# A one-column square root ahead of the last-tile wait in every RMS norm

## What is computed

```
def rms_norm(x, g):
    return x * rsqrt(mean(x*x, axis=-1) + EPS) * g
def ada_norm(x, g, shift, scale):
    return rms_norm(x, g) * (1 + scale) + shift

for layer in 0, 1:
    x += 0.5 * gate * swiglu(ada_norm(x, ...))          # FFN
    x += gate * mixer(ada_norm(x, ...))                 # layer 0: S5 scan, layer 1: gated DeltaNet
    x += 0.5 * gate * swiglu(ada_norm(x, ...))          # FFN
return rms_norm(x, final_g)
```

## Time and profile before

| | |
|---|---|
| median of 3 runs | 2415.01 us |
| lowest, highest | 2410.72, 2417.9 us |
| span of the profiled execution | 2416.0 us |
| TensorE matmul busy | 2139.0 us (89%), 12486 instructions |
| VectorE busy | 1612.0 us (67%) |
| GpSimd busy | 752.2 us (31%) |
| ScalarE busy | 703.8 us (29%), 992 instructions |

### The profile page before, as it was taken

The page is one execution under the profiler, slowest core; times in us unless marked ns, Lnnn a source line. Parts: engine busy times, 40 slices in busy tenths (PEclk is TensorE's granted clock), DMA queues, the critical chain, the costliest instruction groups (busy, mean ns, idle before and its releaser), DMA issues.

```text
span 2416.0 us, 34067 instructions
## 1 busy us (share of the span) xinstructions
PE 2139.0 (89%) x12486; PEld 1810.0 (75%) x12486; DVE 1612.0 (67%) x2255; ACT 703.8 (29%) x992; POOL 752.2 (31%) x588
## 2 busy tenths in 40 slices
PE   3898998982889899999799999869999999788997
PEld 0676777762878588887588888668888888778997
DVE  7867785853434885858885853637777777746555
ACT  1311221221133321212331212324344344324432
POOL 2144663742524120202311212303333223323123
PEclk9999999995679899999999999869999999988999
DMA  7354553639943344444353532211111111003553
GB/s 281 112 219 167 200 196 134 222 126 205 280 127 122 127 169 157 174 140 176 109 201 122 181 132 78 82 35 36 35 35 35 35 35 34 1 18 122 185 181 105
DMA packets 104689, 309.62 MB, mean 128 GB/s; under 512 B 27680, under 2 KB 39456, under 8 KB 95136
## 3 DMA queue, kind: packets, MB, share of 16 engines
q1 hardware_dynamic: 89392, 285.80, 35.3%
q10 hardware_dynamic: 12528, 12.33, 1.7%
q0 software_dynamic: 2688, 10.42, 1.1%
HBM read 280.26 MB, written 28.25 MB: 128 GB/s over the span
## 4 chain that ended last, share of the span: by engine, by line
PE 60%; issue 16%; DVE 10%; POOL 8%; DMA 2%; ACT 1%; SPq 1%; DVEq 1%; ACTq 0%; POOLq 0%
PE PS L219 18%; PE PS L220 17%; PE PS L221 17%; POOL EE L1877 2%; DVE wlo L252 1%; PE PS L1154 1%; POOL DTs L1867 1%; DVE t L920 1%; POOL X L1873 1%; DMA vwS<-vwd 1%; DVE bx L921 1%; PE PS L585 1%; DVE bx L919 1%; DVE rstd L358 1%; PE PS L1027 1%
## 5 line engine op out<-in xcount | busy, mean ns | idle before, releaser
L219 PE MATMUL PS<-hh,whi 128*128 128x512 f32 (+1 forms) x1792 | 662.0, 369 | 46.2 <-DVE hl L376 38.5
L221 PE MATMUL PS<-hh,wlo 128*128 128x512 f32 (+1 forms) x1792 | 653.3, 365 | 0.0
L220 PE MATMUL PS<-hl,whi 128*128 128x512 f32 (+1 forms) x1792 | 653.1, 364 | 0.0
L252 DVE TENSOR_TENSOR wlo<-raw,whi 128x1024 fp32r<-128x1024 f32 x328 | 493.4, 1544 | 94.5 <-ACT whi L246 91.5
L219 PEld LDWEIGHTS PS<-hh,whi 128*128 128x128 f32 x1792 | 342.6, 191 | 124.6 <-issue 56.0
L246 ACT ACTIVATE whi<-raw 128x1024 fp32r<-128x1024 f32 x328 | 329.0, 1051 | 319.7 <-PE PS L221 303.6
L221 PEld LDWEIGHTS PS<-hh,wlo 128*128 128x128 f32 x1792 | 343.1, 191 | 53.1
L220 PEld LDWEIGHTS PS<-hl,whi 128*128 128x128 f32 x1792 | 343.9, 192 | 49.8
L566 POOL CAST hidh<-gt 128x512 f32 (+2 forms) x88 | 59.8, 680 | 905.9 <-DVE gt L515 905.9
L219 PE MATMUL PS<-hidh,whi 128*128 128x512 f32 (+1 forms) x704 | 263.4, 374 | 37.1 <-DVE x L551 26.0
L220 PE MATMUL PS<-hidl,whi 128*128 128x512 f32 (+1 forms) x704 | 260.5, 370 | 0.0
(11 more groups left out here) (298 smaller groups left out, 2946.2 us busy)
## 6 DMA issues: line engine op xcount, KB each, us to landing
modw<-in_mod_w SPq DMA_DIRECT2D x72, 1024.0 KB, 4.8
raw<-in_w_gdn SPq DMA_DIRECT2D x32, 512.0 KB, 4.0
cxd<-cx POOLq DMA_DIRECT2D x16, 576.0 KB, 4.4
cxS<-cxd SPq DMA_DIRECT2D x8, 1152.0 KB, 5.9
raw<-in_w_f0p0a SPq DMA_DIRECT2D x16, 512.0 KB, 6.9
vwd<-vws ACTq DMA_DIRECT2D x16, 512.0 KB, 6.8
raw<-in_w_f0p1a SPq DMA_DIRECT2D x16, 512.0 KB, 6.6
raw<-in_w_glu SPq DMA_DIRECT2D x16, 512.0 KB, 4.2
```

The source lines that it names most:

```text
L219: pe.matmul(dst, w_h, xh, start=first, stop=False)
L220: pe.matmul(dst, w_h, xl, start=False, stop=False)
L221: return pe.matmul(dst, w_l, xh, start=False, stop=last)
L252: dve.tensor_tensor(wlo[:, s, c], raw[:, s, c], whi[:, s, c].bitcast(F32), ALU.subtract)\
```

## The change

Every `norm_act` gets two instructions ahead of its wait for the last tile of `x`: a wait for `mods_ready` to be at least 1 (that is, for `epst` to be written), and a `Sqrt` of the one column of `epst` into a new tile `root_warm` that nothing reads.

```diff
         epst = sb("epst", [P, 1])
+        root_warm = sb("root_warm", [P, 1])
         glub = sb("glub", [P, 2, KT])
...
         def norm_act(act, m):
             layer, n, c0, feeds = NORMS[m] if m < len(NORMS) else (0, 0, CTX, "out")
+            act.wait_ge(mods_ready, 1)
+            act.activation(root_warm[:, :], epst[:, 0:1], ACT.Sqrt)
             if m:
                 for q in range(2):
                     act.wait_ge(x_ready[q], 1 + X_BEFORE[m])
```

## The result

The changed kernel takes 2442.08 us (median of 4 runs, 2441.09 to 2446.06) against 2415.93 us of the kernel before beside it: a ratio of 1.011, 95% interval 1.009 to 1.013. That is 26 us slower where 0.5 us faster was forecast. The profiled execution agrees: its span is 2440.3 us, 24.3 more than the 2416.0 before.

What follows compares the result with a forecast made beforehand. The kernel was taken as bound by matmuls, TensorE carrying 60% of the chain; gains of 0.10, 0.09, 0.10 and 0.22 us summed to 0.51, so 2415.01 - 0.5 = 2414.5 us. The range was 2409.5 to 2419.5 us.

Steps and rivals of the forecast that it cites:

- D: Shift's loop at line 316: a table load in each pass, 18 us slower in all, 2433 us; chance 0.03.
- The norms: Roots of norms 1, 3, 4 and 6 start earlier by 0.10, 0.09, 0.10 and 0.22 us, sum 0.51; others nothing.
- upper bound of 1.7 us: Most the norms could gain if two 512-column matmuls took 0.74 us: 3 x 0.48 + 0.22 us.
- norm 2's idle time: ScalarE ahead of norm 2's square: some 1.0 us idle left after load and root, in place of 2.51.
- norm 0's root: Norm 0: square later, at about 44.5 us, but root where it was, covered by 12.7 us.
- rival B: Norms where the load ended last: the whole load comes off in four, 5.1 us, giving 2409.9 us; chance 0.03.
- its cover: Norm 2: load and root end 1.0 us before the square; 1.5 us lost if this fails.

Runs made afterwards that it cites:

- root_no_tile: Kernel before plus the seven early roots and waits, the root written to a second column of `epst` instead of a new tile; 2416.76 us, ratio 0.9997.
- tile_only: Kernel before plus an unused 4-byte tile declared behind `epst`, with no root and no wait; 2439.47 us, ratio 1.010.
- the sweep: Separate matmul-only kernel, not a change to either kernel, stepping the distance between moving operand and weights; 0.2267 us at 0 bytes, 0.2333 at 32 (512 columns).
- root_two_tiles: Changed kernel plus a second, unused tile declared behind `root_warm`; 2418.32 us, ratio 1.0012 against the kernel before.
- back192_root: Kernel before with the root in a second column of `epst` and the last FFN's four moving operands 192 bytes lower; 2411.91 us, ratio 0.9987.
- back64_root: Kernel before with the root in a second column of `epst` and the last FFN's four moving operands 64 bytes lower; 2406.85 us, ratio 0.9965.

## Why the prediction was wrong

**The wrong step** is the last paragraph of the rivals: "The tiles declared after `epst` move by a few bytes in SBUF. No row prices that; I give it nothing and put it with D's chance." What the runs showed in its place: one unused tile makes the kernel 24.1 us slower. By the estimate it moves the moving operands 32 bytes against their weights, and the 512-column matmuls follow at 0.2333 us in place of 0.2267 (the 256-column ones at 0.1167 in place of 0.1200, which gives 5 us back). It was the only effect of the change that the medians can show. The text saw the move and had no row for it; but it took an unpriced effect for a small one, on an operand of more than 7000 matmuls, in a kernel whose chain is 60% TensorE. At a few ns each the count alone gives tens of us, and that multiplication was open before any run: 3 FFNs of 1584 matmuls make 4752, and 1.5 ns on each are 7 us. The range should have reached there on both sides.

**What D got right and wrong.** Its time, 2433 us, was the nearest to the result, by a mechanism that did not take place: the six loads are where the forecast put them, and the shift's loop holds none. That a forecast of "slower" came near in size is chance.

**The norms.** The steps held, but one bound did not follow. The upper bound of 1.7 us took 0.37 us for the quickest 512-column matmul; that is the mean of a group that mixes 512 and 256 columns (the 512-column ones alone have 0.40), and matmuls overlap, starting 0.2267 us apart, so two of them could be over in 0.2267 + 0.40 = 0.63 us, not 0.74. That makes the bound 2.0 us. Nothing hung on it, as the gain came out at the forecast. The load lay beside TensorE's sum (0.09 us gained in norm 1, 0.21 in norm 6, forecast 0.10 and 0.22). The new root takes 200 ns (forecast 0.22 us), norm 2's idle time fell from 2.51 to 1.00 us as worked out, and norm 0's root did not become later (59.23 us, 59.74 before). The reading that took the chain's 1.23 us for what could be won, rival B, was wrong for the reason given: root_no_tile has all the loads moved, and B's 5.1 us lie outside its interval, whose lower end is 3.9 us. In the changed kernel norm 6 shows a longer wait (2.24 us from square to root); there TensorE's sum waited for GpSimd's until 2427.18 us, so a load behind the square, ending near 2427.8, would not have been last.

**The load in norm 2.** The sigmoid ends at 793.02, the load starts at 793.04 and the new root at 794.33, 1.29 us later, and the square still waits for VectorE. The load took its 1.28 us there and the rows show no pause ahead of it or behind it, so norm 2 kept its cover.

## What to carry to other kernels

An edit that adds a tile can cost more by the tile than by its instructions: here 4 bytes that nothing uses made 24.1 us of loss (tile_only, 2439.47 us), and the seven roots without a tile none that can be measured (root_no_tile, ratio 0.9997). Where matmuls bound the kernel, as here, the pace of TensorE has to be compared before and after, at equal widths (0.2267 against 0.2333 us at 512 columns), before anything is said of the edit itself. To try an edit by itself, do without a new tile, as root_no_tile did with a second column of `epst`, and look whether the pace stayed (0.2267 us there); to learn what the tile is worth, add one that nothing uses. When a difference shows in no engine's waits, cut the execution at an instruction that both kernels have and look which stages grew.

## What the runs showed of the hardware

- With a weight load for each matmul, fp32r operands and a granted clock of 1.00, 512-column matmuls followed each other at 0.2267 to 0.2279 us at the distance of the sweep's first group and 256 or 512 bytes on from it, at 0.2333 with 32 bytes more, at 0.2292 with 64, and at up to 0.2342 with other steps of 32. The slowest, 0.2362, was at 4 bytes. At 256 columns the pace went from 0.1133 us (16 bytes) to 0.1225 (4 bytes); of the 32-byte steps 192 was best (0.1138) and 0 worst (0.1200).
- Moving both by 32 bytes gave nearly the first pace in the sweep (0.2275 us, 0.2267 first; 0.2333 with the weights alone moved). The kernel with a tile ahead of all others kept its pace (0.2267 us, 2417 us); moving both by 16 bytes in the sweep did not give the first pace (0.2300 us).
- At 256 columns two loops of one execution ran at 0.1133 and at 0.1179 us with the same operands (root_two_tiles, by the estimate at 64 bytes), and so at 0.1133 and 0.1178 in back192_root. The distance does not decide between them, and no run tells what does.
- What in the chip makes the pace depend on the distance stays open, and no trace shows the addresses of the kernels' tiles. Open, too, is which of the two weight tiles, `whi` or `wlo`, has to stand well: no run moved one alone.
- Of the 32-byte steps the best is not the same for the two widths: 512 columns have 0.2267 us at 0 bytes and 0.2338 at 192, 256 columns 0.1200 and 0.1138. So none of them gives both their best pace; a shift of the columns in one stage did (back64_root, 2406.85 us with 512 columns at 0 and 256 columns at 192 bytes, counted from the kernel before).
